# Parting the last chunk of an output weight on GpSimd, and moving eight transposes ahead of a product, in a two-block fp32 layer kernel

## What is computed

```
    h = rmsnorm(x, norm_pre[layer])
    proj = h @ w_in[layer]
    pool_u, pool_gate, q, k, v, attn_gate = jnp.split(proj, splits, axis=-1)
    pool_out = pool_mixer(pool_u, pool_w[layer], pool_scale[layer]) * jax.nn.silu(pool_gate)
    attn_out = swa_sink_attention(q, k, v, attn_sinks[layer]) * jax.nn.silu(attn_gate)
    y = jnp.concatenate([pool_out, attn_out], axis=-1) @ w_out[layer]
    x = x + rmsnorm(y, norm_post[layer])
```

## Time and profile before

| | |
|---|---|
| median of three executions | 1674.88 us (1673.2 to 1675.7) |
| the profiled execution | 1673.89 us |
| its span | 1672.1 us |
| granted TensorE clock, mean | 0.998 |
| TensorE (PE) busy | 1653.1 us, 99% |
| VectorE (DVE) busy | 859.1 us, 51% |
| ScalarE (ACT) busy | 566.9 us, 34% |
| GpSimd (POOL) busy | 551.9 us, 33% |

### The profile page before, as it was taken

How to read it: one execution, slowest core, us unless ns; L and a number is a source line. 1 busy time by engine, 2 the same in 40 slices (tenths; PEclk the granted TensorE clock), 3 DMA queues, 4 the chain that set the end, 5 groups by cost and what they waited for, 6 DMA issues and landing times.

```text
span 1672.1 us, 22398 instructions
## 1 busy us (share of the span) xinstructions
PE 1653.1 (99%) x8593; PEld 1370.2 (82%) x8593; DVE 859.1 (51%) x1674; ACT 566.9 (34%) x1323; POOL 551.9 (33%) x482
## 2 busy tenths in 40 slices
PE   9999998999999999999999999999999999999998
PEld 6778786889888788888888887888887999988886
DVE  5430377534352614667076634746503888846713
ACT  5111486434333003440034201431114777741111
POOL 6225176023333333032211133123315645534300
PEclk9999999999999999999999999999999999999999
DMA  5223021332267232112311222146474534226222
GB/s 204 58 73 104 15 68 59 118 110 83 76 235 262 82 117 80 32 48 62 121 59 36 59 79 98 51 142 208 155 237 143 124 77 120 54 80 223 95 113 101
DMA packets 97001, 178.16 MB, mean 107 GB/s; under 512 B 13912, under 2 KB 33792, under 8 KB 96768
## 3 DMA queue, kind: packets, MB, share of 16 engines
q1 hardware_dynamic: 60992, 95.30, 19.6%
q10 hardware_dynamic: 35904, 81.44, 14.0%
HBM read 121.79 MB, written 54.92 MB: 106 GB/s over the span
## 4 chain that ended last, share of the span: by engine, by line
PE 95%; DVE 2%; ACT 1%; DMA 1%; POOL 0%; issue 0%; ACTq 0%; SPq 0%; DVEq 0%; POOLq 0%
PE ps L1282 23%; PE ps L1196 16%; PE ps L905 15%; PE ps L1459 5%; PE ps L1399 5%; PE ps L1132 5%; PE ps L1337 4%; PE ps L1046 4%; PE ps L1429 4%; PE ps L1412 3%; PE ps L964 3%; PE ps L1315 2%; PE ps L1302 2%; PE ps L1098 1%; PE ps L1070 1%; PE ps L943 1%
## 5 line engine op out<-in xcount | busy, mean ns | idle before, releaser
L753 POOL TENSOR_SCALAR w_hi<-w_stage 128x1024 fp32r<-128x1024 f32 (+3 forms) x140 | 127.1, 915 | 816.4 <-PE ps L1282 350.0
L760 POOL TENSOR_TENSOR w_lo<-w_stage,w_hi 128x1024 fp32r<-128x1024 f32 (+3 forms) x140 | 271.8, 1949 | 8.9
L1282 PE MATMUL ps<-h2T_hi,w_hi 128*128 128x512 f32 x384 | 155.9, 406 | 0.6 <-DVE rope_swapped L2437 0.3
L1196 PE MATMUL ps<-h2T_hi,w_hi 128*128 128x512 f32 x384 | 154.1, 401 | 0.3 <-issue 0.3
L1282 PE MATMUL ps<-h2T_hi,w_lo 128*128 128x512 f32 x384 | 152.0, 396 | 0.0
L1196 PE MATMUL ps<-h2T_hi,w_lo 128*128 128x512 f32 x384 | 151.5, 395 | 0.0
L1282 PE MATMUL ps<-h2T_lo,w_hi 128*128 128x512 f32 x384 | 151.4, 394 | 0.0
L1196 PE MATMUL ps<-h2T_lo,w_hi 128*128 128x512 f32 x384 | 151.0, 393 | 0.0
L2437 DVE SCALAR_TENSOR_TENSOR rope_swapped<-ps,sin_table_T 32x512 f32<-32x512 f32 x192 | 131.9, 687 | 3.9
L1860 ACT ACTIVATE probs_dil<-probs_dil,dil_stats_out 128x192 f32<-128x192 f32 (+2 forms) x192 | 84.0, 439 | 94.1 <-DVE dil_stats_out L2465 94.1
L2575 DVE TENSOR_REDUCE small<-ps 128x1 f32<-128x1024 f32 x64 | 77.7, 1214 | 54.9 <-PE ps L1399 54.9
(11 more groups left out here) (310 smaller groups left out, 3802.7 us busy)
## 6 DMA issues: line engine op xcount, KB each, us to landing
w_stage<-in_w_in SPq DMA_DIRECT2D x76, 512.0 KB, 3.9
w_stage<-in_w_out SPq DMA_DIRECT2D x16, 512.0 KB, 3.7
gate_scr<-gate_tiles ACTq DMA_DIRECT2D x16, 512.0 KB, 3.1
gates<-gate_scr ACTq DMA_DIRECT2D x32, 256.0 KB, 3.1
v_dil_scr<-values_out SPq DMA_DIRECT2D x24, 256.0 KB, 2.0
dil_scr<-dil_out SPq DMA_DIRECT2D x96, 64.0 KB, 1.6
dil_nums<-dil_scr ACTq DMA_DIRECT2D x24, 256.0 KB, 4.5
v_dil<-v_dil_scr SPq DMA_DIRECT2D x23, 256.0 KB, 3.2
```

Source lines behind the costliest of these rows:

```text
L753: last = nc.gpsimd.tensor_scalar(hi_, raw_, 1.0, 0.0, ALU.mult, ALU.add)
L760: last = nc.gpsimd.tensor_tensor(lo_, raw_, hi_.bitcast(F32), ALU.subtract)
L1196: m = pe.matmul(ps[:, gate_bank(u), :], a[:, s, k, P * m_:P * m_ + P], b[:, k, COLS * n:COLS * n + COLS], start=(k == 0 and j == 0), stop= ...
L1282: m = pe.matmul(bank, a, b, start=(k == 0 and i == 0), stop=(k == KT - 1 and i == 2))
```

## The change

On GpSimd step 14 (the last but one) no longer stands between chunk 2 and chunk 3 of `o1`; it stands between the high part and the low part of chunk 3. On TensorE, in iteration 15 alone, the transposes of step 14 come ahead of the output product's piece.

```
-    SWA_STEPS = ((7,), (8,), (9,), (10, 11), (12,), (13,), (14,), tuple(range(15, 20)))
+    SWA_STEPS = ((7,), (8,), (9,), (10, 11), (12,), (13,), (), tuple(range(15, 20)))
+    SWA_BETWEEN = 7, 14
...
                     split_high(n + ci, parts)
+                    if p == index["o1"] and ci == SWA_BETWEEN[0] - 4:
+                        swa_step(SWA_BETWEEN[1])
                     split_low(n + ci, parts)
...
             for unit in in_loop.get(i, ()):
                 fill_unit(*unit)
+            if i == steps - 1:
+                swa_transposes(i - 1)
             for unit in out_loop.get(i, ()):
                 out_part(*unit)
-            if 1 <= i <= steps:
+            if 1 <= i <= steps and i != steps - 1:
                 swa_transposes(i - 1)
```

## The result

The changed kernel takes 1676.88 us (median of 20 executions, 1675.78 to 1679.42), the kernel before, timed with it, 1674.14 us (20 executions, 1673.06 to 1675.70). The ratio is 1.0016, 95% interval 1.0010 to 1.0022: 2.7 us slower, where 2.9 us slower was forecast. The time itself came out 0.9 us under the forecast of 1677.8, nearly all of it because the kernel before was 0.7 us faster in the longer comparison than in the three executions that were known. The profiled execution has a span of 1674.5 us against 1672.1.

The account below looks back on a forecast made before the run. TensorE's own work, 95% of the span, was taken as the bound. Order 1.65 plus clock 1.25 gave 2.9 us, on the median of 1674.9 making 1677.8 us, 0.17% slower; range 1674.2 to 1680.3.

Parts of the forecast that it names:

- a later mark: Start of TensorE's value products in iteration 16, 291.34 before: any delay there reaches the kernel's end unless given back.
- rival 4: Later PE waits give the delay back, at most about 1 us: 1675 to 1676, or 1673.7 without a transpose wait; chance 0.09.
- The collision term: GpSimd's moved gate lies across VectorE's L2222, which ends 0.48 us later, putting scaling at 284.15 instead of 283.67.
- the wait is not removed; it changes its releaser and moves ahead of work that was ready: PE waits 2.7 us for L2204 before the transposes, where it did six matmuls and then waited 1.2 us.
- the least certain term: PE's new wait likely brings a second stretch at 1.2 GHz, costing between 0 and 1.6 us, taken as 1.25.
- rival 2: Clock falls vary between executions; one stretch missing and none added gives 1.65 - 1.6 = 0, 1674.9 us; chance 0.12.
- order: Value products start 1.65 us later: 1.29 for six matmuls, 0.30 for the transposes' pace, 0.06 for the wait's later end.

Follow-up runs that it names:

- w2_after_turn: The changed kernel plus the GpSimd wait of w1_turn; 1676.13 us, ratio 1.0008 to the kernel before.
- w9_after_turn_low_first: w2_after_turn with VectorE's low parts of step 13 ahead of the softmax of step 15 in iteration 15; 1672.55 us, ratio 0.9989 to the kernel before.
- w4_after_turn_busy: w2_after_turn plus ten matmuls of unused result ahead of TensorE's transposes of step 14; 1672.57 us, ratio 0.9987 to the kernel before.
- w1_turn: The kernel before plus a GpSimd wait putting VectorE's small operation first at steps 13 and 14; 1673.73 us, ratio 0.9996 to the kernel before.
- e1_pe_only: The kernel before with only TensorE's half of the change, GpSimd's order as before; 1675.15 us, ratio 1.0006 to the kernel before.
- w3_turn_late: w1_turn with step 14 on GpSimd behind the whole of chunk 3; 1671.77 us, ratio 0.9985 to the kernel before.
- w5_late_low_first: w3_turn_late with VectorE's low parts of step 13 ahead of the softmax of step 15 in iteration 15; 1670.06 us, ratio 0.9974 to the kernel before.

## Why the prediction was right

**The bound.** That a later mark is passed on to the end held through the output product (3.0 us) and for 2.4 of them to the end of the profiled executions. Of the other 0.6 us, 0.45 are the slow DMA issue in the profile before, so nothing here speaks for rival 4; the last 0.15 are not traced. Its remark that the waits of this stretch are the largest of the span is not exact: PE waits 1.5 us for VectorE in the first 10 us of the kernel. Nothing hangs on it.

**GpSimd.** The high part went into the idle time, at 280.84 by the old count (280.82 forecast). The gate came at 281.85 (281.84), held L2222, and the scaling came at 284.12 (284.15), the low part at 285.93 (285.96). The collision term, put at 0.48 us, measured 0.44 on VectorE's L2222 and 0.45 on the scaling.

**TensorE.** The transposes had to wait for VectorE's low parts: 289.04 by the old count, forecast 289.10. The step "the wait is not removed; it changes its releaser and moves ahead of work that was ready" is what `w2_after_turn` shows largest, and `w9_after_turn_low_first` shows that there the queue on VectorE is behind it. In the changed kernel as profiled, VectorE's queue is behind less of it. ScalarE's high parts of step 13 came late too:

```profile
287.00 1.08 ACT L1598 ACTIVATE probsT_hi<-ps 128x512 fp32r<-128x512 f32 x2 [3.02 <-PE ps L1101]
```

With its first half done near 287.5, a VectorE that nobody holds would have started its low parts there and not at 288.30, as the working says: an estimated 0.8 of the 2.5 us.

**The clock.** Named as the least certain term, taken at 1.25 us. From 289.04 to the mark took 5.32 us where 3.89 (1.09 + 2.80) was the sum at full clock: 1.43. The mark came 0.12 us behind the forecast 294.24. With the meetings settled a stretch at 1.2 GHz was worth 2.15 us (`w4_after_turn_busy`), above the 1.6 that I gave as its upper end, since in that execution the half clock lasted from 285 to almost 292. But there `w1_turn`, without the change, had such a stretch as well. The clock is a term of the change only where the kernel before keeps its clock through its wait for chunk 3, as it did in the profile that the forecast used.

**What the prediction lacked.** It took one profile for the course of things. That VectorE and GpSimd start within 0.02 us of each other at steps 13 and 14, in rows I had read, and that the order decides over 2 us of PE's time, was not seen; rival 2 put the spread between executions to the clock alone. That the sum did not suffer was luck in part: before and after happened to be profiled with the same outcome. PE's gain from the other outcome also mostly ends in the next wait: settling it brought 0.6 us to the kernel before, and the changed one has 1676.13 with it and 1676.88 without, on different occasions. With the meetings settled the change costs about as much, 2.4 us by the medians, but the parts of the sum are others: some 2.0 of order and 0.1 of clock by the marks, where the forecast had 1.65 and 1.25. The expectation for `e1_pe_only` did suffer, by 2.3 us. That no changed execution of 20 was under 1675.8 is in line with this, but how often each outcome occurs in which kernel was not measured.

## What to carry to other kernels

Before moving work in front of a wait, ask what the moved work waits for itself, and follow that through the queue of the engine that provides it: here the transposes' data were ready and their PSUM banks were not, and what held the banks was VectorE's queue, in it a 128x4 operation that stood for an unrelated one of GpSimd. An in-order engine should get the work that is ready first; putting eight transposes ahead of six ready matmuls left PE idle while they were ready, and in the profile of the changed kernel the longer wait was followed by a stretch at 1.2 GHz as well. Where two engines contend and start within hundredths of a microsecond, compare variants with that order fixed by a wait.

## What the runs showed of the hardware

- A VectorE TENSOR_TENSOR of 128x4 elements with both operands in SBUF takes 0.16 us, and up to 2.37 us when a GpSimd TENSOR_TENSOR is running; it ends with that one. This goes both ways: beside VectorE's two low parts for the output product GpSimd's gate took 1.19 instead of 0.73 us (`w1_turn`) and its high part 1.50 instead of 1.05 us (`w2_after_turn`). The Trainium skill (page "SBUF — State Buffer", section on the two separate sides) gives the rule of whole instructions in turn; the trace agrees.
- VectorE operations that read PSUM kept their times beside both kinds of GpSimd operation: the two of L2204 took 1.28 us together beside a TENSOR_TENSOR (`e1_pe_only`, 270.96) and 1.29 beside a TENSOR_SCALAR (`w9_after_turn_low_first`, 282.67), one of L2185 0.48 us beside either.
- Behind some waits of PE the granted clock was at 1.2 GHz (the 1.87 us wait before, the 2.50 us wait after, the waits of 3.22, 4.43 and 6.23 us), behind others it stayed at 2.4 GHz (2.45 us at 271.2 before, 2.25 us in `w3_turn_late`, 0.87 to 1.29 us in `w5_late_low_first`). With ten unused matmuls in the 6.2 us wait (2.6 us of work between idle times of 2.0 and 1.65 us) it stayed at 2.4 GHz, worth 2.15 us by the mark.
